# Second expert stage: where VectorE makes the next group's weights

## What is computed

```python
act = jax.nn.gelu(jnp.einsum('nd,nhkd->nhk', x_blk, expert_u[i_blk]))
return jnp.einsum('nhk,nhkd->nd', g_blk * act, expert_v[i_blk])
```

## Time and profile before

| | us |
|---|---|
| median of 3 runs | 4740.63 |
| the profiled execution, its own time | 4742.96 |
| span of its trace, first to last instruction | 4740.9 |
| TensorE matmuls busy | 4411.6 (93%) |
| VectorE busy | 2609.1 (55%) |
| GpSimd busy | 2535.9 (53%) |
| ScalarE busy | 1517.6 (32%) |

### The profile page before, as it was taken

The page is one execution under the profiler, slowest core; times in us unless marked ns, Lnnn a source line. Parts: engine busy times, 40 slices in busy tenths (PEclk is TensorE's granted clock), DMA queues, the critical chain, the costliest instruction groups (busy, mean ns, idle before and its releaser), DMA issues. The chain is left out here.

```text
span 4740.9 us, 80533 instructions
## 1 busy us (share of the span) xinstructions
PE 4411.6 (93%) x29778; PEld 4155.7 (88%) x29778; DVE 2609.1 (55%) x4336; ACT 1517.6 (32%) x2325; POOL 2535.9 (53%) x1827
## 2 busy tenths in 40 slices
PE   6899967998779988999999999999899999999999
PEld 5888866886369988999999999999799999999899
DVE  4477764553142211678666666655566666666631
ACT  3122213442143222223333333333333333333242
POOL 5688832322024333345566666667566666666443
PEclk9999978998789999999999999999999999999999
DMA  3222213335934343223589999979888888878532
GB/s 111 72 94 94 95 52 97 110 106 191 408 112 135 122 148 97 78 94 122 169 319 336 325 345 321 345 262 328 299 325 312 322 315 311 322 277 336 214 99 93
DMA packets 360241, 985.55 MB, mean 208 GB/s; under 512 B 43218, under 2 KB 120786, under 8 KB 301170
## 3 DMA queue, kind: packets, MB, share of 16 engines
q1 hardware_dynamic: 275138, 566.67, 35.3%
q0 software_dynamic: 47088, 339.37, 18.5%
q10 hardware_dynamic: 37824, 76.99, 4.2%
HBM read 901.03 MB, written 81.82 MB: 207 GB/s over the span
## 5 line engine op out<-in xcount | busy, mean ns | idle before, releaser
L2578 PE MATMUL val_y_ps<-val_wt,val_v 128*128 128x384 f32 x6144 | 1101.4, 337 | 37.2 <-DVE val_wt L2652 20.8
L2578 PEld LDWEIGHTS val_y_ps<-val_wt,val_v 128*128 128x128 f32 x6144 | 1062.2, 188 | 75.8 <-DVE out_xT L2676 54.0
L248 PE MATMUL rt_acc<-xn_act,rt_w_hi 128*128 128x384 f32 x4096 | 1062.6, 340 | 32.2 <-POOL rt_w_rest L238 31.9
L238 POOL TENSOR_TENSOR rt_w_rest<-rt_w_raw,rt_w_hi 128x512 fp32r<-128x512 f32 x576 | 737.8, 1306 | 507.5 <-ACT rt_w_hi L233 505.1
L2540 POOL TENSOR_TENSOR val_v<-val_v_raw,val_v 128x2048 fp32r<-128x2048 f32 x128 | 590.7, 4615 | 361.3 <-ACT val_v L2611 361.3
L248 PEld LDWEIGHTS rt_acc<-xn_act,rt_w_hi 128*128 128x128 f32 x4096 | 739.2, 188 | 47.2 <-POOL rt_w_rest L238 43.6
L248 PE MATMUL rt_acc<-xn_act,rt_w_rest 128*128 128x384 f32 x2048 | 692.0, 338 | 0.0
L2676 DVE TENSOR_TENSOR out_xT<-out_xT,val_y_ps 128x384 f32<-128x384 f32 x512 | 277.3, 551 | 374.8 <-PE val_y_ps L2578 374.8
L2455 DVE CUSTOM_DVE_ANT_0 rt_space<-rt_space,rt_mid 128x2048 f32<-128x2048 f32 x160 | 360.9, 2281 | 207.8 <-DMA rt_space<-in_peer_u,out_row_id 202.0
L2611 ACT ACTIVATE val_v<-val_v_raw 128x2048 fp32r<-128x2048 f32 x128 | 245.4, 1917 | 584.9 <-PE val_y_ps L2578 546.2
L233 ACT ACTIVATE rt_w_hi<-rt_w_raw 128x512 fp32r<-128x512 f32 x576 | 334.8, 627 | 281.2 <-PE rt_acc L248 194.8
(11 more groups left out here) (404 smaller groups left out, 7376.4 us busy)
## 6 DMA issues: line engine op xcount, KB each, us to landing
rt_w_raw<-in_peer_uT SPq DMA_DIRECT2D x512, 256.0 KB, 5.4
val_v_raw<-in_peer_vp SPq DMA_DIRECT2D x128, 1024.0 KB, 4.8
scan_w_raw<-in_w_in SPq DMA_DIRECT2D x128, 256.0 KB, 3.0
pages_V<-in_cache_v SPq DMA_DIRECT2D x64, 512.0 KB, 12.1
att_w_raw<-in_w_in SPq DMA_DIRECT2D x96, 256.0 KB, 3.2
hid_scratch<-rt_hid ACTq DMA_DIRECT2D x128, 192.0 KB, 6.2
gate_scratch<-rt_space ACTq DMA_DIRECT2D x12, 2048.0 KB, 10.3
val_hid<-hid_scratch SPq DMA_DIRECT2D x32, 768.0 KB, 8.6
```

Of the source, the lines that this page charges most:

```text
L238: e.tensor_tensor(self.rest[:, s, 0:nk, :], self.raw[:, r, 0:nk, :], self.hi[:, s, 0:nk, :].bitcast(F32), ALU.subtract).then_inc(self.rest ...
L248: mm = e.matmul(acc[:, h, 0:width], w[:, s, k, :], act[:, kt0 + k, a, col + h * width:col + (h + 1) * width], start=first and k == 0 and w ...
L2578: mm = e.matmul(y_ps[:, t % 2, 0:DW], v[:, c % 2, a, j, t * P:(t + 1) * P], wt[:, g % 2, j, b, :], start=j == 0 and a == 0 and b == 0, sto ...
```

## The change

In each chunk VectorE's two operations for the next group's weights come behind the addition of the third tile (t = 2), where they came before the addition of the first.

```diff
             def part(g):
                 for c in range(NC):
-                    if g < NG - 1:
-                        for j in range(c // 2 * 2, c // 2 * 2 + 2):
-                            (weight_rest if c % 2 else product)(g + 1, j)
                     due = list(rows_of(g * NC + c))
                     for t in range(CK):
                         e.wait_ge(y_ready, g * KT + c * CK + t + 1 + 2 * CK)
                         x = k.xT[:, c * CK + t, D0:D0 + DW]
                         e.tensor_tensor(x, x, y_ps[:, t % 2, 0:DW], ALU.add).then_inc(y_added, 1)
+                        if t == 2 and g < NG - 1:
+                            for j in range(c // 2 * 2, c // 2 * 2 + 2):
+                                (weight_rest if c % 2 else product)(g + 1, j)
                         if t == 1 and len(due) > 1 or t == CK - 1 and due:
                             row(due.pop(0))
```

## The result

The changed kernel takes 4708.97 us, the median of 4 runs (4706.86 to 4715.25), against 4741.99 for the kernel before (4 runs). The ratio is 0.9932, with a 95% interval of 0.9914 to 0.9949: 32 us faster, 24 to 41 by the interval. The forecast was 47 us. The direction and the mechanism held, and the time lies in the range given for 8 in 10, 4684 to 4714. It lies outside the forecast's own range, 4686 to 4703: 14 us of the gain were missing. The span of the profiled execution is 4708.0 us against 4740.9.

What follows compares the result with a forecast made beforehand. VectorE's late tile addition, with row and weights ahead of it, was taken to hold TensorE 54.0 us. Terms -54.0 + 5.0 + 0 + 1.6 = -47.4 us gave 4693.5 us; own range 4686 to 4703, 8 in 10: 4684 to 4714.

Steps and rivals of the forecast that it cites:

- The boundary between chunks: Next chunk's tile 0 is added with 0.5 us to spare; TensorE's 119 stalls of 0.454 us go: -54.0 us.
- The new place in the chunk: Weights behind tile 2's addition delay no addition TensorE needs, with one row or two: no stall.
- a rule against them: VectorE's next operation starts only when the pipe is empty; 21 one-row groups would stall 0.15 each, 3 us less gain.
- The group's end: Last weights come late in two-row chunk 3 of 9 groups, 0.55 us each: +5.0 us (4.1 to 5.8).
- ScalarE's queue: Weight operations wait later ahead of the `v_raw` copy; with two rows it is 0.55 late but covered: cost 0.
- the prediction's signs: Expected trace after: among others, TensorE's addition waits near 0, nine L2652 waits, ScalarE's `v_raw` waits more than 7.
- SyncE's queue: Later `hid` and `gate` loads, chunk 3's `v_raw` load behind them; eight groups with two rows in chunk 1: +1.6 us (0 to 8).
- my first rival: DMA becomes the bound: queues give only 325 GB/s, chunk 8.53 us, gain 26 us, time 4714; chance 0.12.
- takes its queues in turn: Each DMA engine alternates queues packet by packet; an earlier gather delays `v_raw` by 0.45, eight groups cost 3.6 us more.
- late in every group: Rival: TensorE answers weights at group ends after 0.8 us, not 0.22; 31 groups lose 18 us, 4712; chance 0.06.
- waited for a gather: Rival, slower: gathered rows land late in 34 two-row chunks, holding VectorE and the weights; 4775 at 17.5 us; chance 0.03.
- did what it says: Rival, no effect: the row alone is enough to hold TensorE, time stays 4740; chance 0.05.

Runs made afterwards that it cites:

- e3: The changed kernel with all weights behind tile 1, ahead of the row there, instead of tile 2: 4710.86 us, ratio 0.9929.
- f4: The changed kernel itself measured again, unaltered, in a second series of 5 runs: 4712.49 us, ratio 0.9932.
- e1: The changed kernel with the weights of chunk 3 behind tile 0, those of chunks 0 to 2 still behind tile 2: 4701.51 us, ratio 0.9904.
- e4: The changed kernel with the load of `hid` bringing one of its four parts from group 2 on: 4696.60 us, ratio 0.9906.
- f2: Against the changed kernel: weights behind tile 0, and a group's second gathered row always in chunk 0: 4700.28 us, ratio 0.9907.
- f3: Against the changed kernel: weights behind tile 0, and a group's second gathered row in chunk 1 in nearly every group: 4710.61 us, ratio 0.9925.
- f1: Against the changed kernel: weights behind tile 0, and `gate` loaded one chunk after `hid`, behind chunk 3's `v_raw` load: 4698.18 us, ratio 0.9903.
- e2: The changed kernel with the weights of every chunk behind tile 0 instead of tile 2: 4703.01 us, ratio 0.9907.

## Why the prediction was right in kind and too high by 14 us

- **The boundary between chunks** was right in mechanism: all 119 stalls went. Its size was overstated. In the kernel before, 96 chunks from 3388.40 to 4227.39 take 8.74 us each. In the changed kernel 912 loads take 158.04 us, which is 8.32 for 48. A stall of 0.454 us cost 0.42, because TensorE's loads run a little closer after a rest (8.28 to 8.30 for 48, against 8.32). 119 x 0.4216 = 50.2, not 54.0. The number was to be had: 192 loads in 33.26 us are 8.32 for 48, and the prediction took 8.30.
- **The new place in the chunk** was right: no addition is late, in one-row or two-row chunks. The chunk boundary has its spare time, and e3 confirms the spacings where they were made to fail. (The page "VectorE: DVE Perf Modes" of the Trainium skill, section "The DRAIN you can't avoid", from which the prediction took a rule against them, also says that an operation that is not held starts earlier; the prediction left that out. These rows, 0.47 from start to start for 0.55 us, agree with it.)
- **The group's end** was right: nine gaps, 5.4 us measured, 5.0 predicted. The one-row groups cost nothing, as taken. With the weights at 2.22, as by the rule weighed there, 21 one-row groups would have had gaps; none has.
- **ScalarE's queue** was right in that no copy delayed by the weights alone reaches TensorE. The one gap of 0.36 at 4245.67 lies where ScalarE also copies the 128 finished rows; I had not looked at that place. ScalarE's waits for `v_raw` did not rise in number from 7, as the prediction's signs had it: there are 7, 14.2 us in sum against 35.5, while its weight operations, which stand ahead of the copy, wait longer for VectorE (L2602: 292.9 us, 81.4 before).
- **SyncE's queue is the step that failed**, in the size of the term. I moved the deadline of the `v_raw` load by the two stalls that vanish, 0.9 us, and left its landing as it was: 11.6 us, late by 1.67, covered to 1.30, 0.2 x 8 = 1.6 us, upper end 8. Landing is not a constant. With the period 5% shorter (f4, where all eight landings can be read) it was 11.9 to 14.1 us in the five groups that lose time and 6.4 to 9.6 in the three right behind such a group; before it was 10.7 to 11.6 in all eight. The limit that follows from the prediction, 10.0 + 1.30 = 11.3 us, was right: landings of 14.0, 13.7, 13.6, 11.9 and 14.1 made gaps of 2.77, 2.54, 2.44, 0.73 and 2.97, the excess over 11.3 and 0.1 to 0.2 more, and those below it made none. So what was mis-sized is the landing: 9.3 us of gaps in one trace and 11.5 in the other, where the term was 1.6 and its upper end 8. That it is traffic and not the later issue of `hid` and `gate` is shown by e1 against e4, and where it strikes by f2 against f3. Why the shorter period lengthens the landing by this much no run here takes apart.
- **The stage's start.** The first load came 3.2 us earlier than in the trace before, and the wait behind chunk 0 was 3.2 us longer (3.89 against 0.67). In the other traces it is anything from none (e4, f4) to 4.84 (e1). Up to 3361 the two programs are the same, so I take both for scatter between executions. About 1.5 us more went behind that rest: the granted clock was 0.72 over the next 6 us, 0.50 (the level of 1.2 GHz) in their first half and 1.00 (2.4 GHz) in the second, with 25 matmuls where the kernel before did 34. Three stretches of the changed kernel (us, busy by engine with counts, clock, DMA share, GB/s):

```profile
3376.00:3382.00 6.00, 5.97 (x25) 5.98 (x26) 0.56 (x1) 0.00 (x0) 5.77 (x3) 0.72 0.81 314
3376.50:3379.80 3.30, 3.30 (x12) 3.30 (x12) 0.00 (x0) 0.00 (x0) 3.28 (x2) 0.50 0.80 288
3388.00:3736.00 348.00, 344.91 (x1984) 343.34 (x1983) 243.22 (x301) 116.80 (x124) 241.10 (x94) 1.00 0.84 324
```

Together: -50.2 + 5.4 + 9.3 + 0.4 + 1.5 = -33.6 us; the stage from chunk 1 on is 1108.3 - 1074.6 = 33.7 shorter. The prediction was -47.4, so 3.8 us were lost in the size of a stall, 7.7 in the load's landing, 2.3 in small things. In the second trace (f4) the stage is only 29.7 shorter: the large gaps are 11.5 us, and behind two of them the clock fell, as behind the rest at the start here, for another 3.1 us (see the last section).

**The rivals.** DMA did not become the bound of the whole stage: the third row above has 324 GB/s at a share of 0.84, against 318 before and the 334 that were forecast, and f1 runs the same traffic with no gap at all. It became the bound of a few chunks, which is the case between my first rival and my forecast. That each DMA engine takes its queues in turn, as the page "DMA: Bandwidth & Descriptors" of the Trainium skill says in the section "Queues, rings and completion order", would by the prediction's estimate have added 3.6 us; the measured excess over my term is 7.7. That two gathers at once slow the other queue (f2 against f3) agrees with it; no run here separates the taking of turns from mere volume. The weights were not late in every group, VectorE never waited for a gather, and the change did what it says.

## What to carry to other kernels

When a stall is taken out of a steady loop, every transfer in it gets an earlier deadline and a fuller queue at once; work out both for the latest load of the worst iteration, not for the mean, because only what passes the cover counts, and it counts fully. Look for the iterations in which irregular traffic (here a second gather) meets a periodic burst: moving one of the bursts by an iteration (f1) took away every gap behind the stage's start that was left. Of several legal places for side work on an engine, compute the slack of each consumer for each place; here the place behind tile 0 keeps nobody waiting (in e2 the gaps left are those of the load), and the one behind tile 2 makes TensorE wait at nine group ends.

## What was not expected of the hardware

- A rest of 0.45 us of TensorE costs 0.42: 48 loads behind it take 8.28 to 8.30 us, in a long run 8.32.
- TensorE answers an addition 0.04 us after its end, but the last weight of a group only 0.22 after the earlier trace rows, and again at eight group ends (gaps of 0.62). The ninth, at 4382.30, is the only one that lies outside the hardware loop over groups, and its gap is 0.46, as with 0.04 to 0.06. So it seems to be the loop's waits, whose value comes from a register, that take the 0.2; no run here tests it, and in e3 an addition outside the loop was answered later (0.12) than one inside (0.05).
- A load of 1 MB lands in 4.8 us when nothing is ahead of it on its queue. Behind 1.5 MB more, with one gather beside, it took 6.2 to 8.2 in the kernel before (4.8 in group 25, where no row is gathered at that time), and 10.7 to 11.6 with two gathers beside; with two gathers and the loop 5% faster, 6.4 to 14.1 (f4), long and short in turn.
- A long rest can cost more than itself. Behind the rest of 2.54 us in f4 the granted clock was 0.50, the level of 1.2 GHz, and the next 1008 loads took 176.26 us instead of 174.71; likewise behind 2.97 (f4), 2.60 (e1) and 2.43 (f3). Behind the rest of 2.77 in f4, and of 2.52 in the changed kernel's first trace, it stayed at 1.00. Two stretches of f4, behind the rest of 2.77 and behind that of 2.54 (columns as above):

```profile
3629.50:3632.80 3.30, 3.30 (x19) 3.30 (x20) 0.87 (x2) 0.00 (x0) 3.28 (x2) 1.00 0.74 246
3700.10:3703.40 3.30, 3.30 (x12) 3.30 (x11) 0.56 (x1) 0.00 (x0) 3.30 (x1) 0.50 0.95 397
```
